# First two weight slots of a fused two-block kernel: fewer warm-up products, the second token tile transposed in halves, both gates ahead of two weight splits

## The reference

```python
def swiglu(h, w_gate, w_up, w_down):
    return (jax.nn.silu(h @ w_gate) * (h @ w_up)) @ w_down

hdn = swiglu(rms_norm(x, norm_pre[l, 0]), ffn1_w_gate[l], ffn1_w_up[l], ffn1_w_down[l])
x = x + 0.5 * rms_norm(hdn, norm_post[l, 0])
```

## Time and profile before

| | |
|---|---|
| Time, median of 3 runs | 1692.14 us (1691.43 to 1692.25) |
| The profiled execution | 1690.71 us, span 1688.8 us |
| PE busy | 1674.5 us, 99% of the span |
| DVE, ACT, POOL busy | 69%, 52%, 9% |
| DMA | 359.24 MB, mean 213 GB/s |

### The profile page before, as it was taken

One profiled execution on the slowest core, in us unless ns is written; L12 is line 12 of the kernel. 1 busy time (PEld: TensorE's weight loads), 2 busy tenths in 40 slices (PEclk: granted clock), 3 DMA queues, 4 the chain that ended last, 5 costly groups with the idle time before them and its releaser, 6 DMA issues.

```text
span 1688.8 us, 21662 instructions
## 1 busy us (share of the span) xinstructions
PE 1674.5 (99%) x8388; PEld 1412.2 (84%) x8388; DVE 1163.2 (69%) x1556; ACT 875.3 (52%) x1332; POOL 143.7 (9%) x210
## 2 busy tenths in 40 slices
PE   9999999999999999999999999999999999999998
PEld 7888888888888888888899988888788889888887
DVE  6888776777878667766687675555755568976553
ACT  6555576544544445444466454444544458654442
POOL 0100100000201001010010012000002011310000
PEclk9999999999999999999999999999999999999999
DMA  8877453787749775787554548554666545347551
GB/s 304 321 262 257 161 187 105 246 300 266 272 167 336 255 245 209 254 305 244 189 192 158 183 148 280 187 187 138 223 214 243 189 145 179 123 149 249 186 187 63
DMA packets 99206, 359.24 MB, mean 213 GB/s; under 512 B 11168, under 2 KB 11424, under 8 KB 99104
## 3 DMA queue, kind: packets, MB, share of 16 engines
q1 hardware_dynamic: 92592, 335.59, 58.0%
q0 software_dynamic: 6368, 22.21, 4.1%
q10 hardware_dynamic: 144, 0.07, 0.0%
HBM read 356.70 MB, written 1.12 MB: 212 GB/s over the span
## 4 chain that ended last, share of the span: by engine, by line
PE 90%; DVE 5%; ACT 3%; issue 1%; DMA 1%; POOL 0%; DVEq 0%; POOLq 0%; ACTq 0%
PE gu L452 49%; PE dn L479 28%; PE dn L467 4%; PE gu L467 2%; PE tp L569 2%; DVE w_lo L1630 2%; PE tp L467 1%; PE tp L430 1%; ACT w_hi L1059 1%; DMA raw<-in_weights 1%; ACT arena L1458 0%; DVE x L1658 0%; DVE arena L2047 0%; PE gu L576 0%; PE dn L452 0%
## 5 line engine op out<-in xcount | busy, mean ns | idle before, releaser
L1630 DVE TENSOR_TENSOR w_lo<-raw,w_hi 128x1024 fp32r<-128x1024 f32 x520 | 636.9, 1236 | 317.9 <-ACT w_hi L1059 315.2
L1059 ACT ACTIVATE w_hi<-raw 128x1024 fp32r<-128x1024 f32 x520 | 549.2, 1061 | 470.2 <-PE gu L452 244.3
L452 PE MATMUL gu<-w_hi,hT_hi 128*128 128x512 f32 x1296 | 513.3, 396 | 2.1 <-DVE act_tok L1791 1.0
L452 PE MATMUL gu<-w_lo,hT_hi 128*128 128x512 f32 x1296 | 505.1, 390 | 0.0
L452 PE MATMUL gu<-w_hi,hT_lo 128*128 128x512 f32 x1296 | 504.6, 389 | 0.0
L452 PEld LDWEIGHTS gu<-w_hi,hT_hi 128*128 128x128 f32 x1296 | 243.4, 188 | 53.2 <-DVE w_lo L1630 2.4
L452 PEld LDWEIGHTS gu<-w_lo,hT_hi 128*128 128x128 f32 x1296 | 243.2, 188 | 52.1
L452 PEld LDWEIGHTS gu<-w_hi,hT_lo 128*128 128x128 f32 x1296 | 243.6, 188 | 48.0
L479 PE MATMUL dn<-w_hi,actT_hi 128*128 128x512 f32 x608 | 238.6, 392 | 0.4 <-DVE actT_lo L1638 0.4
L479 PE MATMUL dn<-w_lo,actT_hi 128*128 128x512 f32 x608 | 237.0, 390 | 0.0
L479 PE MATMUL dn<-w_hi,actT_lo 128*128 128x512 f32 x608 | 236.7, 389 | 0.0
(11 more groups left out here) (343 smaller groups left out, 1696.0 us busy)
## 6 DMA issues: line engine op xcount, KB each, us to landing
raw<-in_weights SPq DMA_DIRECT2D x563, 512.0 KB, 4.3
arena<-in_ada_w SPq DMA_DIRECT2D x72, 512.0 KB, 4.3
post_row<-in_post_rows POOLq DMA_DIRECT2D x10, 512.0 KB, 6.3
pre_row<-in_pre_rows POOLq DMA_DIRECT2D x10, 512.0 KB, 6.8
mod_row<-mod POOLq DMA_DIRECT2D x9, 512.0 KB, 9.7
shift_row<-mod POOLq DMA_DIRECT2D x5, 512.0 KB, 9.6
arena<-in_c_rows POOLq DMA_DIRECT2D x2, 512.0 KB, 7.6
arena<-in_ctx_in POOLq DMA_DIRECT2D x1, 1024.0 KB, 10.5
```

The lines of the kernel that those rows point to most:

```text
L452: m = pe.matmul(bank, h[:, k, t * P:(t + 1) * P], w[:, r, kk * 512:(kk + 1) * 512], start=k == 0 and q == 0, stop=k == KT - 1 and q == 2)
L1059: act.activation(o, i, ACT.Copy, **kw).then_inc(done, 1)
L1630: dve.tensor_tensor(w_lo[:, r, :], raw[:, n % RAW, :], w_hi[:, r, :].bitcast(F32), ALU.subtract).then_inc(lo_ready, 1)
```

## The change

PE does 5 and 4 zero matmuls where it did 8 and 5. Tile 1 of `x` is loaded in two halves with a semaphore each, transposed in halves (the first half between slot 0 and slot 1, the second after slot 1) and split in halves between the first slots. ACT's second square moves behind the halves of tile 1. Both gates of step 0 now stand before the splits of slots 7 and 8 on ACT and before those of slots 6 to 8 on DVE.

```diff
-WARM, WARM_ON = 8, 5
+WARM, WARM_ON = 5, 4
...
+            def first_rows(t):
+                for half, done in enumerate((x_half[t], x_loaded[t])):
+                    sp.dma_start(x[:, t, half_of(half)], x_in[bass.ts(t, P), half_of(half)]).then_inc(done, 16)
...
-            sp.dma_start(x[:, 1, :], x_in[P:TOK, :]).then_inc(x_loaded[1], 16)
+            first_rows(1)
...
-                transposed(0, 0)
+                first_turned(0, 0)
+                first_turned(0, 1)
                 keep_warm(WARM_ON)
                 half_there(0, 0)
                 wide_slot(0, 0, {0: gu[:, 0, :]}, used=False)
+                first_turned(1, 0)
+                wide_slot(1, 1, {0: gu[:, 0, :]}, used=False)
                 hT_there(0, 0)
-                transposed(0, 1)
-                wide_slot(1, 1, {0: gu[:, 0, :]}, used=False)
+                first_turned(1, 1)
                 half_there(0, 1)
...
                     gate(0, 0)
-                    upper(7)
+                    upper(6)
                     act.wait_ge(slot_used, 4)
                     gate(1, 1)
+                    upper(7)
                     upper(8)
...
             in_half_upper(0, 0, 1)
             upper(1)
+            in_half_upper(0, 1, 0)
+            upper(2)
+            in_half_upper(0, 1, 1)
             first_squares(1)
-            in_upper(0, 1)
-            upper(2)
             in_squares(0, 1)
-            for n in range(3, 7):
+            for n in range(3, 6):
                 upper(n)
...
                     gated(0, 0, 0)
-                    rest(7)
                     gated(0, 1, 1)
-                    rest(8)
+                    for n in range(6, 9):
+                        rest(n)
...
             rest(1)
-            in_lower(0, 1)
-            for n in range(2, 7):
+            dve.wait_ge(hT_hi_ready, 3)
+            in_half_lower(0, 1, 0)
+            rest(2)
+            dve.wait_ge(hT_hi_ready, 4)
+            in_half_lower(0, 1, 1)
+            for n in range(3, 6):
                 rest(n)
```

More of the change, by code:

```diff
@@ L264, in build @@
         bias_loaded, warm_ready = sem("bias_loaded"), sem("warm_ready")
-        x_half, landed_half, hi_half, lo_half = sem("x_half"), sem("landed_half"), sem("hi_half"), sem("lo_half")
+        x_half = [sem(f"x_half_{t}") for t in range(TT)]
+        landed_half, hi_half, lo_half = sem("landed_half"), sem("hi_half"), sem("lo_half")
         ssq_ready, rstd_ready, x_new, xn_ready = sem("ssq_ready"), sem("rstd_ready"), sem("x_new"), sem("xn_ready")
@@ L388, in ada_load @@
                 sp.dma_start(ada_raw[:, i % ADA_RING, :], ada_w[bass.ts(i, P), :]).then_inc(ada_landed[i % ADA_RING], 16)
-            for half, done in enumerate((x_half, x_loaded[0])):
-                sp.dma_start(x[:, 0, half_of(half)], x_in[0:P, half_of(half)]).then_inc(done, 16)
+            def first_rows(t):
+                for half, done in enumerate((x_half[t], x_loaded[t])):
+                    sp.dma_start(x[:, t, half_of(half)], x_in[bass.ts(t, P), half_of(half)]).then_inc(done, 16)
+            first_rows(0)
             for half, done in enumerate((landed_half, landed[0])):
@@ L419, in _, with in_turned, first_turned @@
         def _(pe):
+            def in_turned(s, t, half, rows):
+                for q in range(4):
+                    k = 4 * half + q
+                    m = pe.transpose(in_bank(s, t, half)[:, q * P:(q + 1) * P], rows[:, t, k * P:(k + 1) * P], ident[:])
+                m.then_inc(hT_psum, 1)
+            def first_turned(t, half):
+                pe.wait_ge(x_loaded[t] if half else x_half[t], 16)
+                in_turned(0, t, half, x)
             def transposed(s, t):
-                if s:
-                    pe.wait_ge(xn_ready, TT * (s - 1) + t + 1)
-                rows = xn if s else x
+                pe.wait_ge(xn_ready, TT * (s - 1) + t + 1)
                 for half in range(2):
[L426 to L431, removed]
+                    in_turned(s, t, half, xn)
             def hT_there(s, t):
@@ L1111, in first_squares @@
             def first_squares(half):
-                act.wait_ge(x_loaded[0] if half else x_half, 16)
+                act.wait_ge(x_loaded[0] if half else x_half[0], 16)
                 square("pre", 0, 0, half, x[:, 0, half_of(half)], 1.0 / D ** 0.5)
```

## The result

| | before | changed |
|---|---|---|
| Median | 1691.12 us (1689.80 to 1692.61, 22 runs) | 1694.07 us (1692.66 to 1696.26, 22 runs) |
| Profiled execution, its span | 1690.71 us, 1688.8 us | 1693.22 us, 1691.3 us |

The ratio is 1.0017, with a 95% interval of 1.0011 to 1.0023. The changed kernel is 2.95 us slower by the medians and 2.5 us by the profiled spans. The forecast was 1694.4 us and +2.3 us. The median of before, now over 22 runs, is 1 us lower than the one that the forecast was added to. The difference is 0.17% of the time: the interval excludes 1, and it lies under the 0.2% that the prediction called slower.

What follows compares the result with a forecast made beforehand. PE, busy 99% of the span, was taken as the bound, meeting step 1's gates without slack near 38.6 us. The 1.9 us lead lost in the pause, +1.3 gates, +1.0 clock: +2.3, 1694.4 us, range 1691.3 to 1695.9.

Steps and rivals of the forecast that it cites:

- The mechanism: Step 0's gates first push back slots 6 and 7, later loads and step 1's gates; PE pauses, its clock may drop.
- Both pauses at slot 4: PE's two waits for act_tok at slot 4, about 1.45 us in all, were to vanish.
- The start: PE's first product at 7.2 us instead of 8.29, 1.1 us earlier; down slots of step 0 end at 36.7.
- The late gates: Step 1's gates start at 37.75 instead of 36.44, costing 1.3 us, with bounds 0 and 2.2.
- The pause: PE idle before step 1's transposes from 36.7 to 39.9, 3.2 us.
- The clock: After the pause before step 1's transposes PE's clock may drop: 1.0 us, taken as half of 2.1.
- full price: The whole cost of a clock fall after the pause at step 1: 2.1 us, read from the kernel's start.
- full-price rival: After 36.7 PE's clock falls and costs 2.1 in full: +3.4 us, 1695.5 us; chance 0.15 for 1695 and up.
- The gates did move: Against the rival that step 1's gates stay at 36.44, set by the weights' DMA: no change, 1692.1 us; chance 0.20.
- the gain did not arrive: Against the rival that step 1's gates come 1.9 us earlier too: 1690.2 us; chance 0.12.
- the shorter warm-up does harm: Rival at the start: clock rises later, PE up to 2 us later at slot 4, some 1 us more; remaining chance 0.01.
- the halves do: Rival: tile 1's load in halves does harm; slots 2 and 3 late by up to 0.5 us; shares the remaining 0.01.

Runs made afterwards that it cites:

- b2: The kernel before with only the new order of gates and splits in step 0: 1693.65 us, 1.70 above the kernel before, ratio 1.0013.
- e2: The changed kernel with both gates of step 1 ahead of slot 12's split on ACT and DVE: 1691.18 us, ratio 1.0000 to the kernel before.
- e1: The changed kernel with eight more matmuls in the pause before step 1's transposes: 1693.99 us, 2.46 above the kernel before, ratio 1.0015.
- f2: The changed kernel with eight more matmuls in PE's pause near 1473 us: 1693.91 us, 2.12 above the kernel before, ratio 1.0013.
- f4: The changed kernel with eight matmuls in the pause before step 1's transposes and eight near 1473 us: 1692.04 us, 1.47 above f1.
- b8: The changed kernel with the warm-up of before (8 and 5 zero matmuls): 1694.19 us, 2.24 above the kernel before, ratio 1.0015.
- b1: The kernel before with only the shorter warm-up (5 and 4 zero matmuls): 1692.00 us, ratio 1.0000.
- b5: The kernel before with seven more matmuls meant for the pause near 1473 us, but placed two down slots beside it: 1693.89 us, 1.94 above, ratio 1.0010.
- f1: The kernel before with eight more matmuls inside PE's pause near 1473 us: 1690.57 us, 1.22 below the kernel before, ratio 0.9994.
- e3: The changed kernel with c_rows loads issued after slot 3's split instead of slot 7's: 1693.68 us, 2.15 above the kernel before, ratio 1.0015.
- e4: The changed kernel with DVE's split of slot 6 back between the two act_tok of step 0: 1692.35 us, 0.82 above the kernel before, ratio 1.0004.
- f3: The changed kernel with step 1's gates ahead of slot 12's split and eight matmuls near 1473 us: 1689.93 us, ratio 0.9990 to the kernel before.

## Why the prediction was right

**The number** of 1694.4 us owes something to luck: the forecast was added to a median of before that is 1 us above the later one. The difference is the fairer test, 2.95 us for a forecast of 2.3.

**The mechanism** was as put down. Both pauses at slot 4 vanished; w_lo of slots 6 and 7 were ready at 22.8 and 24.1 (forecast 22.4 and 23.7), the loads of slots 10 and 11 and c_rows were issued at 22.8, 24.1 and 24.4 (22.4, 23.75, 24.0), the gates came late, and PE paused at the transposes of step 1 and lost its clock. b2 shows that the order of the gates of step 0 is enough to make the pause and the fall, e2 that moving the gates of step 1 is enough to remove them.

**The start** was sized too well: first product at 7.70, not 7.2, and 0.3 us of that are slot 0's halves, which landed at 5.96 and 6.96, later than before. So the down slots ended at 37.26, not 36.7.

**The late gates** cost 0.95 us in the profile for 1.3 forecast. I had slot 11 crowded as before; here it landed at 28.46, and c_rows fell on slots 12 to 14 alone (8.1 to 8.25 us each). But this differs from one execution to the next: in the profiles of e1, f2, f4 and b8, with the same order, slot 11 landed at 30.35 to 31.95. In the five profiles with this order the transposes of step 1 start at 39.13 to 40.47, in four with the order of before (before, b1, b5, f1) at 38.53 to 39.01; the means are 1.15 us apart. Over 11 runs each, with the later pause filled, the term is 1.47. So 1.3 was well sized. Moving c_rows away, as in e3, brings it back through slots 8 and 9.

**The pause** was 2.33 us, not 3.2: PE came 0.56 us later than forecast, and in this execution act_tok 0.4 us earlier.

**The clock** was put at 1.0 as half of 2.1. This is the term that was sized wrong. In the changed kernel's profile it cost 1.64; in those of f2, b2 and b8 the traces lose 1.59, 1.39 and 1.35 over the same matmuls, and the medians of f4 and f2 differ by 1.87. The full price of 2.1 was itself too high: it was read from the start, where the profile's granted clock says 1.00 from 1 to 7 us and only the pace of 0.43 us a matmul speaks for the lower level. The four profiles whose pause at step 1 is 2.3 us or more (2.33, 2.58, 2.61, 2.75) all have the fall; the four with a pause of 0.4 to 1.8 there have none. Half the price was the wrong way to weigh it, and the measured 2.95 lies between the forecast and the full-price rival's 3.4 (the first rival, which the prediction once calls the second). The Trainium skill (TensorE: Matmul & The Clock Gate, "HAM oscillation — how this bites in real kernels") describes such a fall in a kernel whose waits for DMA are some 3 to 5 us. This trace agrees in kind, with a granted clock of 0.50 from 40 to 43 us, and here a shorter pause, of 2.33 us, was enough.

**The rivals.** The gates did move, and the gain did not arrive. That the shorter warm-up does harm by itself fell with b1; that the halves do was not tried alone. What I left out is the fall near 1475 us: seven of the ten profiles without a filling at that pause show it. The one profile of the kernel before does not, but the mean granted clocks of its 33 executions beside f1 suggest that about half of them have it. Each such fall cost 1.6 us in the traces (e1, e2, e4 and the four b runs), and the filling is worth 1.22 us in the median (f1).

## What to carry to other kernels

Where PE is busy in 99% of the span, look for the point at which another chain meets PE without slack, and ask of each reordering what it does to that chain, not only to PE's next wait. Here a wait of 1.45 us on PE was traded for three splits started later, and the DMA-bound chain behind them set the end. A gate or any short link to the bound engine belongs ahead of work that waits for a transfer, if its own inputs are there. And a pause of 2.17 us or more on PE was followed by a fall of the clock in eleven of fourteen cases here, at 1.35 to 1.6 us each beside its own length, so a few idle matmuls in it can pay. They must lie inside the pause: two down slots beside it, in b5, the seven cost 1.9 us.

## What the runs showed that I had not expected

Eight matmuls that do nothing, placed in a pause near 1475 us, took 1.2 us off the median of a kernel of 1691 us, and cut the width of its single times from 3.7 to 1.3 us. The spread between executions of the kernel before was mostly whether the clock fell there, though not every spread is: f3 has the filling too, and two of its eleven executions (1691.42 and 1693.37 us) lie far above the other nine, which are within 1.4 us. Near 1475 us the same pause of 2.17 us was followed by a fall in some profiles and not in others, and I have not found out what decides between them. The loads of slots 12 to 14 took over 8 us beside c_rows, and in 27 to 30 us the queue of c_rows had 80% of the DMA engines; the two queues did not share evenly. What takes 0.75 us from e2 in the attention phase was seen (a pause of 0.73 us at 235 us) but not tried, and f3 does not have it.
